# Taking gate chunks out of PSUM in the fourth unit behind them instead of the first

## The reference, cut to what matters

```python
h = rms_norm(x, norm_gain[l])
proj = jnp.einsum('bsd,dn->bsn', h, w_in[l])
(qa, ka, va, ga, qi, ki, wi, qb, kb, vb, gb, ma, mb) = jnp.split(proj, offsets, axis=-1)
...
p = jax.nn.softmax(jnp.where(valid, s, -jnp.inf), axis=-1)
...
ob = (rms_norm(ob, b_subln_gain[l], SUBLN_EPS) * (1.0 - lambda_init)).reshape(B, S, B_WIDTH)
ya = jnp.einsum('bsc,cd->bsd', oa * jax.nn.silu(ga), w_o_a[l])
yb = jnp.einsum('bsc,cd->bsd', ob * jax.nn.silu(gb), w_o_b[l])
```

## Time and profile before

| | us |
|---|---|
| median of 3 runs | 797.96 (797.94 to 798.95) |
| the profiled execution | 798.46 |
| its span, first to last instruction | 796.6 |
| PE busy | 792.6 (99%) |
| DVE busy | 482.6 (61%) |
| ACT busy | 418.5 (53%) |

### The profile page before, as it was taken

How to read it: one execution, slowest core, us unless ns; L and a number is a source line. 1 busy time by engine, 2 the same in 40 slices (tenths; PEclk the granted TensorE clock), 3 DMA queues, 4 the chain that set the end, 5 groups by cost and what they waited for, 6 DMA issues and landing times.

```text
span 796.6 us, 10771 instructions
## 1 busy us (share of the span) xinstructions
PE 792.6 (99%) x3810; PEld 666.9 (84%) x3810; DVE 482.6 (61%) x663; ACT 418.5 (53%) x670; POOL 46.6 (6%) x70
## 2 busy tenths in 40 slices
PE   9999999999999999999999999999999999999998
PEld 9998888888888888888888888888888888888887
DVE  7687766666677554668656455556455566665453
ACT  7584556665555454556465554555575444443431
POOL 4341000000000000000000000000000000000000
PEclk9999999999999999999999999999999999999999
DMA  9986665666666565666655565656665855555563
GB/s 307 310 268 206 189 184 168 184 196 177 204 187 186 170 196 161 195 188 196 174 155 173 167 175 162 185 160 171 174 186 182 294 194 185 185 191 192 186 194 122
DMA packets 81082, 152.92 MB, mean 192 GB/s; under 512 B 5136, under 2 KB 12944, under 8 KB 80784
## 3 DMA queue, kind: packets, MB, share of 16 engines
q1 hardware_dynamic: 80752, 152.06, 62.8%
q10 hardware_dynamic: 288, 0.30, 0.1%
HBM read 150.25 MB, written 2.10 MB: 191 GB/s over the span
## 4 chain that ended last, share of the span: by engine, by line
PE 97%; ACT 1%; DMA 0%; issue 0%; SPq 0%; DVE 0%; ACTq 0%
PE ps L526 30%; PE ps L528 30%; PE ps L527 29%; PE ps L537 2%; PE ps L568 1%; PE ps L579 1%; DMA raw<-in_w_in 0%; PE ps L637 0%; PE ps L748 0%; PE ps L746 0%; PE ps L747 0%; PE ps L645 0%; ACT L937 0%; ACT L831 0%; ACT g L831 0%; PE ps L625 0%
## 5 line engine op out<-in xcount | busy, mean ns | idle before, releaser
L1067 DVE TENSOR_TENSOR lo<-raw,hi 128x1024 fp32r<-128x1024 f32 (+2 forms) x279 | 336.3, 1209 | 289.3 <-ACT hi L818 287.4
L818 ACT ACTIVATE hi<-raw 128x1024 fp32r<-128x1024 f32 (+2 forms) x277 | 287.1, 1040 | 336.8 <-PE ps L528 324.3
L526 PE MATMUL ps<-hi,hT_hi 128*128 128x512 f32 (+2 forms) x940 | 365.6, 389 | 0.0
L528 PE MATMUL ps<-hi,hT_lo 128*128 128x512 f32 (+2 forms) x940 | 362.5, 386 | 0.0
L527 PE MATMUL ps<-lo,hT_hi 128*128 128x512 f32 (+2 forms) x940 | 362.1, 385 | 0.0
L528 PEld LDWEIGHTS ps<-hi,hT_lo 128*128 128x128 f32 x940 | 176.4, 188 | 35.4
L527 PEld LDWEIGHTS ps<-lo,hT_hi 128*128 128x128 f32 x940 | 176.6, 188 | 32.9
L526 PEld LDWEIGHTS ps<-hi,hT_hi 128*128 128x128 f32 x940 | 176.5, 188 | 32.8
L526 PE MATMUL ps<-hi,ogT_hi 128*128 128x512 f32 x128 | 50.0, 391 | 0.0
L528 PE MATMUL ps<-hi,ogT_lo 128*128 128x512 f32 x128 | 49.8, 389 | 0.0
L527 PE MATMUL ps<-lo,ogT_hi 128*128 128x512 f32 x128 | 49.8, 389 | 0.0
(11 more groups left out here) (167 smaller groups left out, 478.7 us busy)
## 6 DMA issues: line engine op xcount, KB each, us to landing
raw<-in_w_in SPq DMA_DIRECT2D x192, 512.0 KB, 3.8
raw<-in_w_out SPq DMA_DIRECT2D x32, 512.0 KB, 3.6
raw<-in_w_o_a SPq DMA_DIRECT2D x16, 512.0 KB, 3.7
raw<-in_w_o_b SPq DMA_DIRECT2D x16, 512.0 KB, 3.6
raw<-in_w_in SPq DMA_DIRECT2D x13, 384.0 KB, 5.2
raw<-in_w_in SPq DMA_DIRECT2D x8, 336.0 KB, 5.3
x_own<-in_x SPq DMA_DIRECT2D x4, 512.0 KB, 6.2
g<-in_x SPq DMA_DIRECT2D x1, 2048.0 KB, 9.9
```

What stands on the lines that cost most here:

```text
L526: mm(o, a_hi, w_hi[:, j], start=first and j == 0, stop=False)
L528: ins = mm(o, a_lo, w_hi[:, j], start=False, stop=j == 1 and last)
L818: activation(hi[:, slot, :, 0:width], raw[:, slot, :, 0:width], ACT.Copy).then_inc(hi_ready, 1)
L1067: tt(lo[:, slot, :, 0:width], raw[:, slot, :, 0:width], hi[:, slot, :, 0:width].bitcast(F32), ALU.subtract).then_inc(lo_ready, 1)
```

## The change

ACT takes chunks 16, 17 and 18 out of PSUM in the fourth unit of the next chunk (i == 3) and not in the first (i == 0). All other chunks stay where they were. DVE's wait ahead of the gate product follows suit: heads 0 to 3, whose gate lies in chunk 15, wait for that chunk alone, heads 4 to 7 for chunk 16 as before.

```diff
@@ -945,7 +945,7 @@
             for c in range(C_V, C_O):
                 for i in range(CK):
                     u = c * CK + i
-                    if i == 0:
+                    if i == (3 if C_G + 1 < c <= C_M else 0):
                         if c == C_V:
                             qk_chunk(c - 1, chunk_bank(c - 1))
                         elif c <= C_G:
@@ -1257,7 +1257,7 @@
                             dve.wait_ge(heads_psum, h + 1)
-                            dve.wait_ge(chunk_out, C_G + 2)
+                            dve.wait_ge(chunk_out, C_G + 1 + h // 4)
                             settle()
```

## The result

The changed kernel takes 801.84 us (median of 6 runs, 799.99 to 803.01) against 798.03 us for the kernel before (median of 6 runs): a ratio of 1.0045, 95% interval 1.0035 to 1.0055. It is slower by 3.8 us and lies in the stated range, 1.5 us above the predicted 800.3. It is within 0.2 us of the first rival's 801.7, in which PE's clock falls.

The account below looks back on a forecast made before the run. It took PE, busy for 99% of the span, to bound the kernel. Its terms, -0.66 + 0 + 0 + 2.97 = +2.31 us, added to 797.96 gave 800.3 us, range 799.7 to 802.2.

Parts of the forecast that it names:

- first rival: PE's clock falls in the 2.7 us gap at head 5's transpose: +1.4 us, so 801.7 us; chance 0.23.
- What bounds the kernel: PE is busy for 99% of the span; work of ACT or DVE counts only if PE waits for it.
- Part 1: SiLUs and loads gone ahead of heads 2 and 4: both PE stalls at line 645 go, -0.66 us.
- Part 2: Moved work in chunks 17 and 18: high part some 0.15 us late, hidden by later slack, taken as 0.
- Part 3: Two added table loads of 1.28 us each: ACT pays 2.6 us in its idle time, counted as 0.
- that rival: A table switch in the new place hides a further pause of 1.3 us, making 801.6 us; chance 0.04.
- Part 4: In chunk 19 DVE's gain product waits for chunk 18, delaying head 5's transpose by 2.87 us; PE loses 2.97 us.
- Unit (19, 5): PE's unit in chunk 19 needs a low part from DVE, expected in time with 0.47 us to spare.
- the sum: All terms added, -0.66 + 0 + 0 + 2.97 = +2.31 us, giving 800.3 us.
- the chain by itself: The hand-made chain of some ten links behind 800.3 us, with its own range of 799.9 to 800.7.

Follow-up runs that it names:

- e4: The changed kernel with both gain products moved from chunk 19 to chunk 20, so DVE does not wait for chunk 18 in chunk 19; 797.27 us.
- e9: The kernel before with only the two gain products moved to chunk 20, no chunk's eviction moved; 798.05 us.
- e6: The changed kernel with chunk 18 put back to the first unit, so chunks 16 and 17 alone are moved; 797.88 us.
- e1: The changed kernel measured again without any edit, as reference for the other runs on its chip; 802.36 us.
- e2: The changed kernel with ten unused matmuls of 512 columns on PE ahead of its wait for head 5's exponentials; 800.54 us.
- e5: The kernel before with chunk 18 alone moved to the fourth unit; 802.41 us.
- e8: The changed kernel with chunk 18 taken in the fifth unit instead of the fourth; 803.78 us.
- e3: The changed kernel with the second gain product moved from step (19, 2) to (19, 5), out of DVE's chain; 799.26 us.

## Why the prediction was right in its chain of waits and short by the clock

**What bounds the kernel** held: PE loses every microsecond that it waits, and nothing given away by ACT or DVE is seen until PE waits. The signs that the prediction named came: one wait of 3.1 us at line 645, a gain product that waits 6.41 us, eight table loads, 25.02 us for chunk 18. But so did its sign for the first rival, a clock below 1.00 behind the gap and more than 28.5 us: chunk 19 took 29.38 at 0.94, where the forecast had 28.0.

**Part 1, -0.66 us,** is shown: both waits are gone in e4, and the stretch is 0.62 us shorter than in e9, which differs from it in nothing else; e6 shows the half. Against the trace before it is 0.79, but e9, in which PE's waits are those of before, is also 0.17 below it, so that much has another source, most likely the scatter of single traces.

**Part 2, nothing,** is shown by the window of chunk 18 in the changed kernel (25.02) and by e4.

**Part 3, nothing,** is shown likewise. The load in its new place takes 1.28 us (432.93 to 434.21) and the SiLU starts at 434.23, so the drain that the Trainium skill's page "ScalarE: Activation LUTs" (section "What ACT_TABLE_LOAD costs") adds is not there in the new place either, and that rival is out.

**Part 4, +2.97 us,** is shown to the hundredth in its main piece: the transpose is 2.87 us late in the changed kernel, e1 and e2, 2.86 in e5, and 1.74 for a forecast 1.73 when a product of DVE is taken out. Unit (19, 5) did not stop, as the 0.47 us to spare had said.

**The step that fell short** is the sum, which has no term for the clock. I had the clock's fall as a rival with a chance of 0.23, and it is the common case, in 14 of 16 runs with this gap. The time lies in the range only because the range was stretched for that rival; the chain by itself had 799.9 to 800.7.

The rival's price was right by luck: 1.4 us was a guess of half a unit, since no row showed how long the lower level lasts. The traces show 3.4 us, in which a matmul takes 0.43 us for 0.23 (1.9 times, not twice), and a price of 1.46 and 1.58. With 1.46 the sum is -0.66 + 2.97 + 1.46 = +3.77, and 3.8 was measured. So close an agreement is partly chance too: the median is over runs whose clock was down for different lengths, and in the two runs with the clock whole the time rose by 1.96 (changed kernel, 799.99) and 2.77 (e5, 800.75) where the sums without the clock were 2.31 and 2.64.

A row that spoke for the rival was in front of me: the clock fell 2.3 us after the last matmul's end, and I had worked out a gap of 2.7. It could not have settled the matter, since the same gap left the clock whole in 2 of 16 runs. My reason against, that the gap stands between dense stretches, has no row behind it.

The rule of the Trainium skill's page "TensorE: Matmul & The Clock Gate" (section "HAM oscillation — how this bites in real kernels"), that gaps in PE's work are paid again in a slower clock behind them, agrees with the traces of the changed kernel and e1. The waits in its example are longer and repeated; here a single idle stretch of 2.71 us was enough in most runs, and not in the traced one of e5.

## What to carry to other kernels

When an eviction is put off, look not only at who waits for the bank but for every wait on the same counter, and read what is queued behind that wait on its engine: here one gain product waited, and head 5's maximum three steps down the list paid. Then compare any new gap in TensorE's work with the shortest silence after which the trace shows the clock falling, and if it is longer, put the slow stretch into the sum rather than among the rivals, unless its end falls into time in which PE waits anyway (e8). Where such a gap cannot be closed, matmuls without purpose in it can cost nothing and keep the clock: e2's transpose came no later than e1's, and the kernel took 1.8 us less.

## What the runs showed of the hardware that was not expected

- A single idle stretch of 2.71 us between dense matmuls was followed by a clock of 1.2 GHz in most executions, not in all: of the 16 runs of the changed kernel (6), e1 (5) and e5 (5), 14 have a mean clock below 1.000. In the 11 runs of e3, with 1.58 us, and the 6 of e2, with 0.45 us behind ten matmuls, it never fell.
- The same gap had three outcomes in three traces. In the changed kernel the clock fell in the gap (443.81, 2.6 us after the last matmul's end at 441.22). In e1 it fell 1.4 us after PE had started again (444.33, 4.1 us after the end at 440.22). In e5 it did not fall. What decides between them, no run here shows.
- Once down, it was down for 3.4 us in each of the three traces that have it (changed kernel, e1, e8), whatever the moment of its fall. That cost 1.46 and 1.58 us, and nothing in e8, where PE had a second wait behind it.
- Some runs have a mean clock of 0.995 instead of 0.998. In the changed kernel, e1 and e5 they are among the slowest (802.61 to 803.21); in e8 one is the fastest (803.54) and one the slowest by far (806.28). A mean of 0.995 over 800 us is some 7 to 9 us at the lower level, more than two stretches of 3.4 (an estimate). None of these runs was traced, so whether their slow stretch is longer or comes more than once stays open.
